# Sorted mixture-of-experts turns in three capacities instead of two, and weight rows laid out four to a partition

## The chip, the cores and the metric

The kernel runs on one core of one Trainium2 chip. The metric is the device time of one launch in microseconds. Three runs of the kernel before took 1242.91, 1248.9 and 1250.15 us (median 1248.9). The one profiled execution took 1235.75 us.

## The reference

Two trunk layers over 384 tokens (128 of context, 256 latent) of width 1024, in float32. Each layer has a mixer (gated linear attention and mLSTM in layer 0, a Hyena long convolution in layer 1), and after it a hierarchical mixture of experts. Only that second half changes here:

```python
g_logits = u @ moe_w_group + b                    # 4 groups, top 1
e_logits = u @ moe_w_router + b                   # 16 experts, top 2 inside the group
hg = einsum('bld,edf->blef', u, moe_w_gate)       # per expert 1024 x 512
hu = einsum('bld,edf->blef', u, moe_w_up)         # per expert 1024 x 512
h  = silu(hg) * hu * gates
out = einsum('blef,efd->bld', h, moe_w_down)      # per expert 512 x 1024
```

Each of the 768 (token, choice) pairs of a layer lands on one of 16 experts. The reference's router, evaluated on its own inputs, gives these counts. Layer 0: experts 0 to 2 have 44, 44, 71; the other thirteen, sorted, 96, 84, 74, 72, 62, 47, 43, 41, 38, 22, 16, 7, 7. Layer 1: 39, 58, 74; sorted 85, 69, 67, 49, 49, 46, 42, 39, 38, 37, 30, 30, 16.

## The kernel before, in words

**Turns.** A layer's mixture is 16 turns `p`, one expert each. Turns 0 to 2 are experts 0 to 2 with room for 96 rows (`CAP`). The other 13 experts are sorted on the chip by their count (L1674 to L1677), and `RANK_AT` says which rank has which turn. Ranks 0 to 5 have 96 rows, ranks 6 to 12 have 64 (`CAP2`). A turn is cut into tiles of 32 rows: 3, 3, 3, then 3, 2, 3, 2, 3, 2, 3, 2, 3, 2, 3, 2, 2, which is 41 tiles a layer. Should an expert have more rows than room, all engines take a slow branch (`over > CAP`) that recomputes every expert; with the counts above neither layer takes it.

**Rows.** VectorE works out the row of each pair (L1674 to L1698), GpSimd scatters the token rows to `x_rows` in HBM (L885) and reads each turn's rows back (L893). The layer's first weights behind the ones loaded ahead are asked for once rows of turn 1 and of turn 2 are in SBUF (L662, L663).

**A tile on TensorE.** `gate_up` (L2258) does 32 matmuls in each of two halves of 16: stationary 128 x 32 (transposed token rows), moving 128 x 256 (128 columns of gate and 128 of up), with four column groups of the array side by side. `hidden_t` transposes the hidden tile of the tile before, `down` (L2284) does 16 matmuls with 256 moving columns for it. A matmul has two records in the profile, so 32 records are one half of `gate_up`, or one `down`. `rows_t` (L2247) transposes the next turn's rows in between. ScalarE and VectorE evacuate and apply silu.

**Weights.** One expert is 2 MB each of gate, up and down, through a ring of slots in SBUF. SyncE's queue issues them (`step`, L654): in step `p`, when the last `gate_up` of turn `p` is done, gate and up of turn `p + 2`, then a down load three turns ahead while `p < AHEAD`, none at `p == AHEAD` (5), and two ahead after it; then `store(p)` writes the turn's results to `y_rows` in HBM. All these go through one hardware queue, in order. Gate and up have contiguous 16 KB of HBM per partition; down is read as `(k p) n`, four separate rows of 4 KB per partition (L426).

**The end of a layer.** In layer 0 TensorE does `first_taps(0)` (L2193, the Hyena filter's first tap; it needs the 1 MB load `w3`, L707 to L710) ahead of the last `hidden_t` and `down`. All results are stored, GpSimd gathers each token's two rows (L903), and they are combined beside the filters (L1570 to L1584 on VectorE, L2205 on TensorE). In layer 1 the last turn stays in SBUF: a selection matrix (`pick`, made by `in_last` and `pick_table`) adds it in a matmul (`last_expert`, L2419), and the gather waits for the stores of turns 0 to 14 only (L900); its second half lands in `uT`, which also holds down weights of every third turn, 14 among them.

Of the kernel before, what the change touches and what calls it, by code (L numbers as in the profile page):

```python
# [35 lines left out]
CAP, CAP2 = 96, 64  # L36
# [3 lines left out]
HALF = RANKS // 2  # L40
AHEAD = 5
RANK_AT = [None] * FIXED + [0, 6, 1, 7, 2, 8, 3, 9, 4, 10, 5, 11, 12]
CAPS = [CAP if r is None or r < HALF else CAP2 for r in RANK_AT]
BASES = [p * CAP if r is None else FIXED * CAP + r * CAP - max(r - HALF, 0) * (CAP - CAP2) for p, r in enumerate(RANK_AT)]
ROWS = sum(CAPS)
TILES = [c // 32 for c in CAPS]
# [64 lines left out]
def build(nc, A, O):  # L111

    ctx = ExitStack()
    with ctx:
# [419 lines left out]
        pick = work[:, 3840:3840 + NT * 2 * P].rearrange("p (j i t) -> p j i t", j=NT, i=2)  # L534
        pick_rows = work[:, 4608:4608 + NT * 2 * P].rearrange("p (j n) -> p j n", j=NT)
# [78 lines left out]
        def _(sp):  # L614
# [18 lines left out]
            def moe_loads(l):  # L633
# [77 lines left out]
                store(NE - 2)  # L711
                if l == 0:
                    store(NE - 1)
# [5 lines left out]
            def overflow_sp(l):  # L719
                sp.wait_ge(S("overflow_flag"), l + 1)  # L720
                over = sp.value_load(flag[0:1, 0:1], min_val=0, max_val=T + CAP - CAP2)
                with sp.If(over > CAP):

                    for i in range(TILES[NE - 1]):
                        evacuated(sp, (l, NE - 1, "Y", i))
# [37 lines left out]
        def _(pool):  # L763
# [113 lines left out]
            def moe(l):  # L877
# [30 lines left out]
                over = pool.value_load(flag[0:1, 0:1], min_val=0, max_val=T + CAP - CAP2)  # L908
# [43 lines left out]
        def _(act):  # L952
# [173 lines left out]
            def moe(l):  # L1126
# [47 lines left out]
                for p in range(1, NE):  # L1174
                    for i in range(TILES[p]):
# [7 lines left out]
                        if i == 1 and l == 1 and p in KEEP_AT:  # L1183
# [3 lines left out]
                        if i == 1 and l == 1 and p in PICK_AT:  # L1187
                            n = PICK_AT.index(p)
                            full(act, ("pick", n))
                            free(act.copy(pick[:, n, :, :], bank(("pick", n))[:, 0:2 * P].rearrange("p (i t) -> p i t", i=2)), ("pick", n))  # L1190
                rows_out(NE - 1, TILES[NE - 1] - 1)
                act.wait_ge(S("overflow_flag"), l + 1)
                over = act.value_load(flag[0:1, 0:1], min_val=0, max_val=T + CAP - CAP2)
# [68 lines left out]
        def _(v):  # L1262
# [355 lines left out]
            def moe(l):  # L1618
# [60 lines left out]
                v.tensor_scalar(small[:, FIXED:], rank, float(HALF), float(CAP - CAP2), ALU.is_ge, ALU.mult)  # L1679
                v.tensor_scalar(base[:, FIXED:], rank, float(CAP), float(FIXED * CAP), ALU.mult, ALU.add)  # L1680
                chain(v.tensor_scalar(late, rank, -float(HALF), 0.0, ALU.add, ALU.max))
                chain(v.scalar_tensor_tensor(base[:, FIXED:], late, -float(CAP - CAP2), base[:, FIXED:], ALU.mult, ALU.add))
# [33 lines left out]
                def in_last(q):  # L1716
                    chain(v.tensor_scalar(here[:, q, :], at2[q], float(BASES[NE - 1]), None, ALU.is_ge))
# [4 lines left out]
                    chain(v.scalar_tensor_tensor(slot[:, q, :], at2[q], -float(BASES[NE - 1]), here[:, q, :], ALU.add, ALU.mult))  # L1722
# [4 lines left out]
                def pick_table():  # L1727
                    chain(v.tensor_tensor(slot[:, 0, :], slot[:, 0, :], slot[:, 1, :], ALU.add))
                    chain(v.tensor_tensor(wl[:, 0, :], wl[:, 0, :], wl[:, 1, :], ALU.add))
                    local = bc(iota[:, 0:2 * 32].rearrange("p (i s) -> p i s", i=2).unsqueeze(2), [P, 2, 4, 32])  # L1730
                    for j in range(NT):
                        v.tensor_scalar(pick_rows[:, j, :].rearrange("p (i q s) -> p i q s", i=2, q=4), local,
# [26 lines left out]
                for p in range(1, NE):  # L1759
                    for i in range(TILES[p]):  # L1760
# [5 lines left out]
                        if i == 1 and p < NE - 1:  # L1766
                            rows_in(p + 1)
# [8 lines left out]
                over = v.value_load(flag[0:1, 0:1], min_val=0, max_val=T + CAP - CAP2)  # L1776
# [115 lines left out]
        def _(pe):  # L1892
# [328 lines left out]
            def moe(l):  # L2221
# [36 lines left out]
                def gate_up(p, i, half):  # L2258
# [67 lines left out]
                for p in range(1, NE):  # L2326
                    for i in range(TILES[p]):
# [7 lines left out]
                        if i == 1 and l == 1 and p in KEEP_AT:  # L2335
# [3 lines left out]
                        if i == 1 and l == 1 and p in PICK_AT:  # L2339
                            n = PICK_AT.index(p)  # L2340
                            pe.wait_ge(S("final_rows"), 1)
                            transposes(("pick", n), [(t * P, pick_rows[:, n, t * P:(t + 1) * P]) for t in range(2)])
# [7 lines left out]
                over = pe.value_load(flag[0:1, 0:1], min_val=0, max_val=T + CAP - CAP2)  # L2350
                with pe.If(over > CAP):
                    for i in range(TILES[NE - 1]):
                        evacuated(pe, (l, NE - 1, "Y", i))
                    with pe.Fori(0, NE * OVF) as n:
# [11 lines left out]
                        for k in range(4):  # L2366
                            ins = pe.transpose(ps[4][:, k * P:(k + 1) * P], hov[:, k * P:(k + 1) * P], ident)
# [180 lines left out]
```

## Time and profile before

| | us |
|---|---|
| median of 3 runs | 1248.9 |
| profiled execution | 1235.75 |
| its span | 1233.9 |
| TensorE matmul busy | 1148.7 (93%) |
| VectorE busy | 377.4 (31%) |
| ScalarE busy | 219.6 (18%) |
| DMA mean rate | 276 GB/s |

The span is 1.85 us shorter than the execution. Busy TensorE is not TensorE at its peak, since matmul records overlap. The mixture's stretches are about 352 to 628 us (layer 0) and 938 to 1212 us (layer 1).

### The profile page before, as it was taken

The numbers are of one execution on the slowest core, as the hardware profiler recorded it, in microseconds if no ns is written. First come the engines' busy times: TensorE is split into PE (matmuls) and PEld (weight loads), VectorE is DVE, ScalarE is ACT, GpSimd is POOL, SyncE is SP. The second block draws the span as 40 slices with busy tenths as digits, with TensorE's granted clock in tenths as the row PEclk, the third lists the DMA queues.
The fourth block names the chain that finished last, engine by engine and source line by source line (L and its number), as shares of the span: only waits on it lengthen the run. The fifth ranks groups of instructions, "written<-read, shape, count | busy, mean of one in ns | idle before, by whom it ended". The sixth has DMA issues, their size and how long they took to land.

```text
span 1233.9 us, 25011 instructions
## 1 busy us (share of the span) xinstructions
PE 1148.7 (93%) x10971; PEld 641.6 (52%) x10971; DVE 377.4 (31%) x962; ACT 219.6 (18%) x465; POOL 141.4 (11%) x163
## 2 busy tenths in 40 slices
PE   5899999899989998988999999999998999998997
PEld 2443445555565554544546665545666555554555
DVE  3201332574341111101157222587624121110114
ACT  2002201321221111111124111121022111111112
POOL 1043100022120000000020000042232000000001
PEclk9899999899999998999999999999999999999999
DMA  9988855359659999999947301001485999999994
GB/s 381 397 299 286 328 201 209 141 166 407 243 208 375 400 403 361 371 399 399 406 141 271 102 36 69 1 0 69 172 354 207 379 398 399 364 374 407 397 371 163
DMA packets 74716, 340.96 MB, mean 276 GB/s; under 512 B 6898, under 2 KB 17681, under 8 KB 59820
## 3 DMA queue, kind: packets, MB, share of 16 engines
q1 hardware_dynamic: 62872, 300.98, 63.0%
q0 software_dynamic: 11248, 37.99, 8.9%
q8 instruction: 88, 1.44, 0.5%
q10 hardware_dynamic: 484, 0.35, 0.1%
q14 instruction: 24, 0.20, 0.1%
HBM read 315.02 MB, written 24.27 MB: 275 GB/s over the span
## 4 chain that ended last, share of the span: by engine, by line
PE 70%; DMA 19%; DVE 5%; issue 2%; ACT 2%; POOL 1%; SPq 1%; POOLq 0%; DVEq 0%; ACTq 0%
PE ps L2272 18%; PE ps L1983 17%; DMA ring<-in_moe_w_up 13%; PE ps L1905 13%; PE ps L2296 6%; PE ps L2496 3%; DMA ring<-in_ada_w 3%; PE ps L1926 3%; PE ps L2205 2%; PE ps L2466 1%; PE ps L1898 1%; PE ps L2255 1%; PE ps L2282 1%; ACT work L1145 1%; DMA x_rows<-work 1%
## 5 line engine op out<-in xcount | busy, mean ns | idle before, releaser
L2272 PE MATMUL ps<-ring,work 128*32 128x256 f32 x5248 | 329.6, 395 | 35.2 <-DMA ring<-in_moe_w_up 31.6
L2272 PEld LDWEIGHTS ps<-ring,work 128*32 128x32 f32 x5248 | 165.7, 113 | 144.1 <-issue 48.4
L1983 PE MATMUL ps<-uT,ring 128*128 128x384 f32 x640 | 214.2, 491 | 2.4 <-DVE uT L1333 1.3
L1983 PEld LDWEIGHTS ps<-uT,ring 128*128 128x128 f32 x640 | 120.2, 191 | 86.4 <-issue 8.0
L2296 PE MATMUL ps<-ring,work 128*32 128x256 f32 x1792 | 106.7, 379 | 0.8 <-DVE work L1751 0.8
L1751 DVE COPY work<-ps 128x128 f32<-128x128 f32 x82 | 23.8, 290 | 254.5 <-PE ps L2282 254.4
L1157 ACT ACTIVATE work<-ps 128x128 f32<-128x128 f32 x82 | 22.8, 278 | 348.2 <-PE ps L2272 348.2
L1905 PE MATMUL ps<-ring,uT 128*128 128x512 f32 x192 | 84.1, 595 | 0.0
L2296 PEld LDWEIGHTS ps<-ring,work 128*32 128x32 f32 x1792 | 57.6, 110 | 39.4 <-DVE work L1751 1.1
L1747 DVE TENSOR_TENSOR work<-ps,work 128x128 f32<-128x128 f32 x82 | 23.9, 291 | 168.7 <-ACT work L1157 168.7
L1836 DVE SCALAR_TENSOR_TENSOR work<-ps,vecT,work 128x127 f32<-128x127 f32 x96 | 35.5, 411 | 91.6 <-ACT work L1240 90.7
L893 POOL DMA_DIRECT2D work<-x_rows x30 | 15.6, 519 | 417.0 <-PE ps L2255 407.2
L1905 PEld LDWEIGHTS ps<-ring,uT 128*128 128x128 f32 x192 | 35.9, 190 | 47.2 <-issue 47.2
L1926 PE MATMUL ps<-ring,silc 128*32 128x512 f32 x384 | 51.2, 668 | 6.4 <-DMA ring<-in_ada_w 5.1
L1163 ACT COPY work<-ps 128x256 f32<-128x256 f32 x82 | 30.5, 372 | 121.9 <-PE ps L2296 121.9
L2496 PE MATMUL ps<-uT,ring 128*128 128x384 f32 x128 | 43.3, 492 | 1.2 <-DVE uT L1883 1.2
L1905 PE MATMUL ps<-work,ring 128*128 128x128 f32 (+3 forms) x256 | 39.7, 293 | 1.5 <-DVE ring L1870 0.8
L1898 PE MATMUL ps<-tab_common,work 128*128 128x128 f32 (+2 forms) x161 | 25.3, 288 | 14.9 <-DMA work<-in_t_pos 11.1
L2296 PE MATMUL ps<-uT,work 128*32 128x256 f32 x624 | 38.4, 379 | 0.0
L1905 PEld LDWEIGHTS ps<-work,ring 128*128 128x128 f32 (+1 forms) x256 | 32.5, 190 | 8.9 <-PE ps L1905 2.5
L931 POOL TENSOR_TENSOR ring<-ring 128x1024 f32<-128x1024 f32 x4 | 13.6, 3403 | 204.1 <-DVE ring L1859 204.1
L1905 PE MATMUL ps<-work 128*128 128x512 f32 x80 | 35.4, 593 | 0.0
(348 smaller groups left out, 1074.4 us busy)
## 6 DMA issues: line engine op xcount, KB each, us to landing
ring<-in_moe_w_gate SPq DMA_DIRECT2D x32, 2048.0 KB, 11.8
ring<-in_moe_w_up SPq DMA_DIRECT2D x32, 2048.0 KB, 16.6
ring<-in_ada_w SPq DMA_DIRECT2D x24, 2048.0 KB, 11.1
ring<-in_moe_w_down SPq DMA_DIRECT2D x22, 2048.0 KB, 19.1
uT<-in_moe_w_down SPq DMA_DIRECT2D x10, 1536.0 KB, 19.4
ring<-in_rec_w_in SPq DMA_DIRECT2D x6, 2048.0 KB, 24.2
ring<-in_hy_w_in SPq DMA_DIRECT2D x6, 2048.0 KB, 11.2
y_rows<-work SPq DMA_DIRECT2D x72, 96.0 KB, 13.6
```

The costliest lines, as they stand in the source:

```text
L1163: free(act.copy(ysb[:, p % 2, i, :], bank((l, p, "Y", i))[:, 0:256]), (l, p, "Y", i))
L1747: free(v.tensor_tensor(hh[:, par, :], bank((l, p, "GU", i))[:, P:2 * P], sg[:, par, :], ALU.mult), (l, p, "GU", i))
L1751: free(v.tensor_copy(hT[:, (FIRST[p] + i) % 2, :], bank((l, p, "HT", i))[:, 0:P]), (l, p, "HT", i))
L1836: ins = v.scalar_tensor_tensor(dst[:, a0 + do:a0 + do + n], src[:, a0 + so:a0 + so + n], w, dst[:, a0 + do:a0 + do + n], ALU.mult, ALU.add)
L1898: ins = pe.transpose(bank(key)[0:n, at:at + p], src, ident[0:p, 0:p])
L1905: ins = pe.matmul(out, lhsT, rhs, start=(i == 0), stop=(i == n - 1))
L1926: ins = pe.matmul(bank(key)[32 * q:32 * q + 32, :], silc[:, 2 * two + k, :], w[:, k, q * 512:(q + 1) * 512], start=(two == 0 and k == 0), ...
L1983: ins = pe.matmul(bank(key)[0:rows, 0:T], w(k), uT[:, k, :], start=(k == 0), stop=(k == DC - 1))
L2205: done(pe.matmul(bank(key)[:], h2T[:, j * P:(j + 1) * P], w3[0:65, at:at + 512], start=True, stop=True), key)
L2272: ins = pe.matmul(bank(key)[32 * q:32 * q + 32, 0:2 * P].rearrange("p (a n) -> p a n", a=2), xg[:, u, k, 32 * i:32 * i + 32], ring[:, 3 * ...
L2296: ins = pe.matmul(bank(key)[32 * q:32 * q + 32, 0:256], hT[:, (FIRST[p] + i) % 2, 32 * k:32 * k + 32], w[:, q * 256:(q + 1) * 256], start= ...
L2496: ins = pe.matmul(bank(("ho", m))[:, 0:T], w[:, k, (m % 4) * P:(m % 4 + 1) * P], uT[:, k, :], start=(k == 0), stop=(k == DC - 1))
```

## The change

Three capacities: ranks 0 to 4 have 96 rows, ranks 5 to 9 have 64, ranks 10 to 12 have 32. The turns' tiles become 3, 3, 3, then 3, 2, 1, 3, 2, 3, 2, 3, 2, 3, 2, 1, 1: 37 a layer. `AHEAD` goes from 5 to 4. In layer 1 the last two turns (one tile each) stay on chip, the gather waits for turns 0 to 13, and its second half lands in ring slot 5. In layer 0 `first_taps(0)` moves behind the last `down`. VectorE gets four more small instructions in the rank arithmetic. The down load takes four consecutive rows per partition (`(p k) n`); the hidden units then have to stand in another order, so each of the four column groups of `gate_up` takes every fourth weight column, a moving operand with a step of 4 float32 (16 bytes).

```diff
-CAP, CAP2 = 96, 64
+CAP, STEP = 96, 32
-AHEAD = 5
-RANK_AT = [None] * FIXED + [0, 6, 1, 7, 2, 8, 3, 9, 4, 10, 5, 11, 12]
+SMALLER = (5, 10)
+AHEAD = 4
+RANK_AT = [None] * FIXED + [0, 5, 10, 1, 6, 2, 7, 3, 8, 4, 9, 11, 12]
+def rank_cap(r):
+    return CAP - STEP * sum(r >= n for n in SMALLER)
+PICKED = (NE - 2, NE - 1)
...
-            return A["moe_w_down"][l, e].rearrange("(k p) n -> p k n", p=P)
+            return A["moe_w_down"][l, e].rearrange("(p k) n -> p k n", p=P)
...
-        last_rows = [utok, uT.rearrange("p k t -> p (k t)").rearrange("p (j d) -> p j d", j=NT)]
+        last_rows = [utok, ring[:, 5, 0:NT * D].rearrange("p (j d) -> p j d", j=NT)]
...
-                store(NE - 2)
                 if l == 0:
-                    store(NE - 1)
+                    for p in PICKED:
+                        store(p)
...
-                        pool.wait_ge(S(f"y{u}_stored"), 4 * 16 * (NE // 2 * (l + 1) - u * l))
+                        pool.wait_ge(S(f"y{u}_stored"), 4 * 16 * (NE // 2 * (l + 1) - l))
...
-                v.tensor_scalar(small[:, FIXED:], rank, float(HALF), float(CAP - CAP2), ALU.is_ge, ALU.mult)
+                v.tensor_scalar(small[:, FIXED:], rank, float(SMALLER[0]), float(STEP), ALU.is_ge, ALU.mult)
+                v.tensor_scalar(above[:, 1, :], rank, float(SMALLER[1]), float(STEP), ALU.is_ge, ALU.mult)
+                v.tensor_scalar(above[:, 2, :], rank, -float(SMALLER[1]), 0.0, ALU.add, ALU.max)
...
+                v.tensor_tensor(small[:, FIXED:], small[:, FIXED:], above[:, 1, :], ALU.add)
+                chain(v.tensor_tensor(late, late, above[:, 2, :], ALU.add))
...
                         for q in range(4):
-                            at = k * DE + q * P
+                            w = ring[:, 3 * u:3 * u + 2, k * DE:(k + 1) * DE].rearrange("p a (n c) -> p a c n", c=4)
                             ins = pe.matmul(bank(key)[32 * q:32 * q + 32, 0:2 * P].rearrange("p (a n) -> p a n", a=2),
-                                            xg[:, u, k, 32 * i:32 * i + 32], ring[:, 3 * u:3 * u + 2, at:at + P],
+                                            xg[:, u, k, 32 * i:32 * i + 32], w[:, :, q, :],
                                             start=(k == 0), stop=(k == DC - 1))
...
+                hidden_t(NE - 1, TILES[NE - 1] - 1)
+                down(NE - 1, TILES[NE - 1] - 1)
                 if l == 0:
                     loaded(pe, "w3")
                     pe.wait_ge(S("sin_out"), 2)
                     first_taps(0)
-                hidden_t(NE - 1, TILES[NE - 1] - 1)
-                down(NE - 1, TILES[NE - 1] - 1)
...
-                    for i in range(2):
-                        evacuated(pe, (l, NE - 1, "Y", i))
+                    for p in PICKED:
+                        evacuated(pe, (l, p, "Y", 0))
                     def last_expert(j):
-                        for i in range(2):
+                        for i, p in enumerate(PICKED):
                             for q in range(4):
...
-                                          ysb[32 * q:32 * q + 32, (NE - 1) % 2, i, :], start=(i == 0), stop=False)
+                                          ysb[32 * q:32 * q + 32, p % 2, 0, :], start=(i == 0), stop=False)
```

## Rows read from the trace of the kernel before

**Rows 1.** The page: busy time of the engines.
```profile
PE 1148.7 (93%) x10971; PEld 641.6 (52%) x10971; DVE 377.4 (31%) x962; ACT 219.6 (18%) x465; POOL 141.4 (11%) x163
```

**Rows 2.** TensorE's waits, 352 to 625 us: engine, line, releaser: total, times, longest.
```profile
PE ps L2272 <- DMA ring<-in_moe_w_up: 16.7, 6, 3.6
```

**Rows 3.** Windows, layer 0: busy us of each engine, TensorE clock, DMA share, GB/s.
```profile
393.00:398.00 5.00, 5.00 (x89) 2.66 (x81) 0.29 (x1) 0.85 (x2) 0.00 (x0) 1.00 1.00 429
402.00:404.00 2.00, 2.00 (x39) 1.12 (x37) 0.29 (x1) 0.00 (x0) 0.00 (x0) 1.00 1.01 410
404.50:407.50 3.00, 3.00 (x64) 1.70 (x54) 0.29 (x1) 0.56 (x2) 0.00 (x0) 1.00 1.04 314
...
490.00:495.00 5.00, 5.00 (x93) 3.02 (x93) 0.58 (x2) 0.65 (x2) 0.00 (x0) 1.00 0.61 168
```

**Rows 4.** Timeline of TensorE, layer 0: start, us, line, instruction, [idle before].
```profile
473.33 3.64 PE L2272 MATMUL ps<-ring,work 128*32 128x256 f32 x32 [3.56 <-DMA ring<-in_moe_w_up]
...
477.31 2.67 PE L2272 MATMUL ps<-ring,work 128*32 128x256 f32 x32
...
591.96 1.93 PE L2272 MATMUL ps<-ring,work 128*32 128x256 f32 x32
...
597.56 1.91 PE L2272 MATMUL ps<-ring,work 128*32 128x256 f32 x32
...
603.64 1.93 PE L2272 MATMUL ps<-ring,work 128*32 128x256 f32 x32
```

**Rows 5.** Timeline of SyncE's queue, layer 0.
```profile
369.49 0.34 SPq L637 DMA_DIRECT2D ring<-in_moe_w_gate  x1
...
607.76 0.57 SPq L630 DMA_DIRECT2D ring<-in_hy_f_w  x1
```

**Rows 6.** DMA issues: what, queue, count, KB each, median us to landing.
```profile
ring<-in_hy_f_w SPq DMA_DIRECT2D x1, 1024.0 KB, 15.3
```

**Rows 7.** The chain of waits, end of layer 0: start, us, what.
```profile
611.90 3.62 PE ps L2272 x32
...
615.77 1.86 PE ps L2272 x32
...
626.53 1.93 PE ps L2296 x32
628.46 1.80 PE ps L2193 x4
630.27 5.35 PE ps L2205 x12
```

**Rows 8.** The chain of waits, end of layer 1.
```profile
1196.31 3.26 PE ps L2272 x32
...
1207.85 0.99 POOL work L903
...
1218.48 1.15 PE ps L2426 x4
```

**Rows 9.** Timeline of VectorE: the rank arithmetic of layer 0.
```profile
348.08 0.17 DVE L1679 TENSOR_SCALAR work<-work 128x13 f32<-128x13 f32 x1
348.17 0.17 DVE L1680 TENSOR_SCALAR work<-work 128x13 f32<-128x13 f32 x1
...
348.44 0.17 DVE L1682 SCALAR_TENSOR_TENSOR work<-work 128x13 f32<-128x13 f32 x1
```

**Rows 10.** Instructions by line, ns min/median/max: small reductions, and copies by ScalarE.
```profile
L1646 DVE TENSOR_REDUCE work<-work x2: 237/238/240, 338.6 to 923.2; 128x12 f32<-128x48 f32 x2
...
L1694 DVE TENSOR_REDUCE work<-work x4: 202/203/203, 351.2 to 936.0; 128x3 f32<-128x48 f32 x4
...
L1145 ACT ACTIVATE work<-ps,work x12: 1115/1134/1159, 337.0 to 925.6; 128x512 f32<-128x512 f32 x12
...
L1119 ACT COPY ring<-ps x24: 567/585/586, 636.5 to 853.0; 128x512 f32<-128x512 f32 x24
```

**Rows 11.** The matmuls of `gate_up` in the same view.
```profile
L2272 PE MATMUL ps<-ring,work x5248: 376/379/637, 352.9 to 1206.9; 128*32 128x256 f32 x195
```

More of the change, by code:

```diff
@@ L39 @@
 RANKS = NE - FIXED
-HALF = RANKS // 2
-AHEAD = 5
-RANK_AT = [None] * FIXED + [0, 6, 1, 7, 2, 8, 3, 9, 4, 10, 5, 11, 12]
-CAPS = [CAP if r is None or r < HALF else CAP2 for r in RANK_AT]
-BASES = [p * CAP if r is None else FIXED * CAP + r * CAP - max(r - HALF, 0) * (CAP - CAP2) for p, r in enumerate(RANK_AT)]
+SMALLER = (5, 10)
[3 more added lines that the diff above has]
+    return CAP - STEP * sum(r >= n for n in SMALLER)
+CAPS = [CAP if r is None else rank_cap(r) for r in RANK_AT]
+BASES = [p * CAP if r is None else FIXED * CAP + sum(rank_cap(n) for n in range(r)) for p, r in enumerate(RANK_AT)]
 ROWS = sum(CAPS)
+PICKED = (NE - 2, NE - 1)
+assert all(CAPS[p] == 32 for p in PICKED) and BASES[PICKED[0]] == ROWS - 64
 TILES = [c // 32 for c in CAPS]
@@ L720, in overflow_sp @@
                 sp.wait_ge(S("overflow_flag"), l + 1)
-                over = sp.value_load(flag[0:1, 0:1], min_val=0, max_val=T + CAP - CAP2)
+                over = sp.value_load(flag[0:1, 0:1], min_val=0, max_val=T + len(SMALLER) * STEP)
                 with sp.If(over > CAP):
-                    for i in range(TILES[NE - 1]):
-                        evacuated(sp, (l, NE - 1, "Y", i))
+                    for p in PICKED:
+                        evacuated(sp, (l, p, "Y", 0))
                     sp.nop().then_inc(S(f"over{l}_y_stored"), 16)
@@ L907, in moe @@
                 pool.wait_ge(S("overflow_flag"), l + 1)
-                over = pool.value_load(flag[0:1, 0:1], min_val=0, max_val=T + CAP - CAP2)
+                over = pool.value_load(flag[0:1, 0:1], min_val=0, max_val=T + len(SMALLER) * STEP)
                 with pool.If(over > CAP):
@@ L1182, in moe @@
                             rows_in(p + 1)
-                        if i == 1 and l == 1 and p in KEEP_AT:
+                        if i == min(1, TILES[p] - 1) and l == 1 and p in KEEP_AT:
                             n = KEEP_AT.index(p)
@@ L1186, in moe @@
                             free(act.copy(x_tok[:, n // 2, n % 2 * 512:(n % 2 + 1) * 512], bank(("xk", n))[:]), ("xk", n))
-                        if i == 1 and l == 1 and p in PICK_AT:
+                        if i == min(1, TILES[p] - 1) and l == 1 and p in PICK_AT:
                             n = PICK_AT.index(p)
                             full(act, ("pick", n))
-                            free(act.copy(pick[:, n, :, :], bank(("pick", n))[:, 0:2 * P].rearrange("p (i t) -> p i t", i=2)), ("pick", n))
+                            free(act.copy(pick[:, n, :, :], bank(("pick", n))[:, 0:len(PICKED) * P].rearrange("p (i t) -> p i t", i=len(PICKED))), ("pick", n))
                 rows_out(NE - 1, TILES[NE - 1] - 1)
                 act.wait_ge(S("overflow_flag"), l + 1)
-                over = act.value_load(flag[0:1, 0:1], min_val=0, max_val=T + CAP - CAP2)
+                over = act.value_load(flag[0:1, 0:1], min_val=0, max_val=T + len(SMALLER) * STEP)
                 with act.If(over > CAP):
@@ L1716, in in_last @@
                 def in_last(q):
-                    chain(v.tensor_scalar(here[:, q, :], at2[q], float(BASES[NE - 1]), None, ALU.is_ge))
+                    chain(v.tensor_scalar(here[:, q, :], at2[q], float(BASES[PICKED[0]]), None, ALU.is_ge))
                     chain(v.tensor_scalar(slot[:, q, :], at2[q], float(ROWS), None, ALU.is_ge))
@@ L1721, in in_last @@
                     chain(v.tensor_tensor((w1, w2)[q], (w1, w2)[q], wl[:, q, :], ALU.subtract))
-                    chain(v.scalar_tensor_tensor(slot[:, q, :], at2[q], -float(BASES[NE - 1]), here[:, q, :], ALU.add, ALU.mult))
+                    chain(v.scalar_tensor_tensor(slot[:, q, :], at2[q], -float(BASES[PICKED[0]]), here[:, q, :], ALU.add, ALU.mult))
                     chain(v.tensor_tensor(here[:, q, :], at2[q], here[:, q, :], ALU.mult))
@@ L1765, in moe @@
                         hidden(p, i)
-                        if i == 1 and p < NE - 1:
+                        if i == min(1, TILES[p] - 1) and p < NE - 1:
                             rows_in(p + 1)
@@ L1775, in moe @@
                 v.wait_ge(S("overflow_flag"), l + 1)
-                over = v.value_load(flag[0:1, 0:1], min_val=0, max_val=T + CAP - CAP2)
+                over = v.value_load(flag[0:1, 0:1], min_val=0, max_val=T + len(SMALLER) * STEP)
                 with v.If(over > CAP):
@@ L2334, in moe @@
                             rows_t(p + 1, i)
-                        if i == 1 and l == 1 and p in KEEP_AT:
+                            if TILES[p] == 1:
+                                rows_t(p + 1, 1)
+                        if i == min(1, TILES[p] - 1) and l == 1 and p in KEEP_AT:
                             n = KEEP_AT.index(p)
@@ L2338, in moe @@
                             transposes(("xk", n), [(m * P, xT[:, 4 * (n % 2) + m, j * P:(j + 1) * P]) for m in range(4)])
-                        if i == 1 and l == 1 and p in PICK_AT:
+                        if i == min(1, TILES[p] - 1) and l == 1 and p in PICK_AT:
                             n = PICK_AT.index(p)
                             pe.wait_ge(S("final_rows"), 1)
-                            transposes(("pick", n), [(t * P, pick_rows[:, n, t * P:(t + 1) * P]) for t in range(2)])
+                            transposes(("pick", n), [(t * P, pick_rows[:, n, t * P:(t + 1) * P]) for t in range(len(PICKED))])
+                hidden_t(NE - 1, TILES[NE - 1] - 1)
+                down(NE - 1, TILES[NE - 1] - 1)
                 if l == 0:
@@ L2366, in moe @@
                         for k in range(4):
-                            ins = pe.transpose(ps[4][:, k * P:(k + 1) * P], hov[:, k * P:(k + 1) * P], ident)
+                            ins = pe.transpose(ps[4][:, k * P:(k + 1) * P], hov.rearrange("p (n c) -> p c n", c=4)[:, k, :], ident)
                         ins.then_inc(S(f"over{l}_ht"), 1)
```

15 lines of the change are left out of this document (8 added, 7 removed).

## The prediction

> **What bounds the kernel now.** I read the page first: TensorE is busy 93% of the span [rows 1], which makes fewer matmuls look like the whole story. Inside a mixture it is not. TensorE's waits show six stops of up to 3.6 us, 16.7 us in all, for the up load in layer 0 [rows 2], and the windows show why: with weights flowing the DMA engines are busy throughout [rows 3]. A tile takes 5.60 us (597.56 less 591.96) and one with a row transpose 6.08 us (603.64 less 597.56) [rows 4]. A pair of turns with five tiles is then about 30 us of TensorE, while its two experts are 12.6 MB, 30 us at 410 to 429 GB/s, and about 1.3 MB of token rows on top, 3 to 4 us. So from the first issue at 369.49 us [rows 5] to the landing of the last up load, at which TensorE starts turn 15 at 611.90 and 1196.31 us [rows 7, 8], the queue of loads sets the pace. I call this landing T. Only what stands behind T is TensorE's and the gather's own.
>
> **Fewer tiles.** Four fewer per layer, eight in all, at 5.60 us are 45 us of TensorE time. Ahead of T nearly all of it turns into longer waits for weights. What is left of it there is traffic: a tile is 32 rows of 4 KB, 0.13 MB read and 0.13 MB written. Four reads and two writes fewer stand ahead of T (the turns up to 13 go from 37 to 35 tiles), 0.79 MB; such rows travel in stretches like 404.5 to 407.5 us, at 314 GB/s [rows 3]: **2.5 us** a layer.
>
> **The gap.** Between 490 and 495 us the rate is 168 GB/s [rows 3], since step 5 issued no down load and the queue ran dry: 5 x (1 - 168/429) = 3.0 us. Now the pause is at step 4, and turn 5 has one tile, so that its slots are free some 12 us sooner and the queue is full when the pause bites. Turn 6 has three tiles and may leave a gap of a microsecond where the queue was short. I take **2.0 us** a layer; bounds 0 and 3.0.
>
> **The down load.** Gate and up (16 KB in a row per partition) run at 429 GB/s, a stretch of down alone (4 KB rows) at 410 [rows 3]. 2.1 MB are 5.11 us at the one and 4.89 at the other, 0.22 us a load; twelve down loads of a layer stand between the first issue and T, 2.7 us, of which I take **2.0**, since the first turns are TensorE's. Below: 0. Above: the stretch where down and token rows mix, 3 us at 314 GB/s, would go at 429 too, 0.8 us more a turn, 9.6 us a layer. I stay near the row of down alone, because that mix contains rows that do not change. The price could be a longer wait of the token rows behind packets four times as long; they are asked for more than a turn before their use, which is the cover.
>
> Together T comes 6.5 us earlier. Layer 1 has the same turns and I take the same: **13.0 us**.
>
> **Behind T, layer 0.** Now turn 15 has two tiles, with `first_taps(0)` between; filters start at 630.27, T + 18.4 [rows 7]. After the change TensorE is through with one tile at about T + 10 (3.6 for the first half and up to 2.7 for the second [rows 4, 7], 1.9 [rows 7] for each of the downs of turns 14 and 15, and some tenths of waiting for VectorE that no other matmul covers any more). But `first_taps(0)` needs `w3`, issued at 607.76 and 15.3 us under way [rows 5, 6], so landed at T + 11.2. It stands behind the last down load in the same queue and comes no sooner against T. From there the taps and three VectorE instructions take about 3 us (an estimate from the 1.80 us of taps [rows 7] and about as much of VectorE), so filters start at T + 14.3: **4.0 us**. The stores and the gather move by more and are no longer last.
>
> **Behind T, layer 1.** The chain runs over down of turn 14, its store, the gather (first at 1207.85, T + 11.5) and ends where TensorE takes the gathered rows, 1218.48, 10.6 us after the gather began [rows 8]. Now the gather needs turn 13's store alone. That is issued ahead of T but queues behind the last down load, 5 us behind T, so it lands at about T + 6.5 and the gather starts at T + 7.3, its rows are there at T + 17.9 instead of T + 22.2: **4.3 us**. TensorE, with a tile less, is there before. Its clock can be low: it will have stood for some 9 us before T, and after a wait of 3.56 us the two halves took 3.64 and 2.67 us [rows 4] against 1.93. These 2.5 us are in the T + 10 above.
>
> **VectorE.** Four more instructions on 128 x 13 values ahead of the row numbers, one of them in the chain: 0.09 us for one that follows the one ahead (348.17 less 348.08), and 0.19 for one in the chain (the 0.27 from 348.17 to 348.44 less one such) [rows 9], 0.46 us a layer, and the scatter, the rows and so the first issue wait for it: **0.9 us lost**. The other edits of constants and the gather's destination cost nothing that a row shows. No turn overflows: the counts of the reference fit 96, 64 and 32, the tightest being 30 in 32.
>
> **The sum.** 13.0 + 4.0 + 4.3 - 0.9 = 20.4 us. The profiled execution would go from 1235.75 to 1215.4. It lies below all three timed runs; on their median of 1248.9 the forecast is **1228 us**.
>
> **The step of four.** This sum takes the strided moving operand at no cost. No matmul of the trace has one. Half a `gate_up` takes 1.86 us on the chain [rows 7] (1.93 in the timeline, which counts the overlap [rows 4]), a record 379 ns [rows 11], with the moving columns in a row. The nearest rows are of other engines: a reduction of 48 values read with a step of 4 takes 238 ns, and 203 with a step of 1, though it also writes 12 values instead of 3; ScalarE's write of 512 values scattered by 512 bytes takes 1134 ns, a plain copy 585 [rows 10]. So the ends are 0 and twice. I take 0 because a float32 matmul goes over its columns slowly: 32 records of 256 columns, four groups side by side, in 1.86 us are 0.9 ns a column and record, so an operand read has that long, and TensorE has slack besides: 37 tiles at 5.60 and 30 row transposes at 0.48 make 222 us in a stretch of 276 (352.9 to 628.46 [rows 7, 11]). An extra microsecond a tile is hidden but for the three tiles ahead of the first issue and the last one.
>
> The Trainium skill speaks against this change here: Advanced Engine Details and Errata, section SBUF Cachelines, says that a 16-byte line wants at least two hits to absorb the SRAM's latency and that a different line on every access costs. A step of 4 float32 is one hit a line. By this rule the sum has a penalty in all 74 tiles, of a size that the page does not state; the rows on VectorE and ScalarE agree with it, none shows it for TensorE.
>
> **Rivals.**
> - *The strided read is slow* (slower than before). Place: all of `gate_up`. If each element costs what the reduction suggests, 35 ns over 48 values or 0.7 ns, a column and record go from 0.9 to 1.6 ns, and a tile's 3.72 us (twice 1.86) become 6.6: 37 x 8.5 + 15 + 5 of waits = 333 us a layer against 276, 57 more, twice: about **1363 us**. At twice the time, 37 x 9.3 + 20 = 364: about **1425**. It decides from `gate_up` about a third longer: (276 - 227)/37 = 1.3 us of 3.72. For it: both rows. Against: the time that a float32 column has. Chance 0.20.
> - *A small cost, mostly hidden.* Half a microsecond to one a tile: 4 exposed tiles a layer, 4 to 8 us lost: about **1234**. Chance 0.08.
> - *T does not move*, because the queue loses its time elsewhere (token rows behind long packets, a gap at turn 6): only the ends count, 7.4 us: about **1241**. For it: the rate dips at every turn to 314. Chance 0.14.
> - *It does not do what it says*: a count over 32 in rank 10 takes the slow branch, far above the range. The margin is two rows. Chance 0.02.
> - The forecast: 0.56, its own range 1214 to 1240 (bounds of down load and gap, and 0.6% between runs).
>
> **How the numbers follow.** About 12 us, 1%, is what can be told from no change here. Faster by more: 0.50 of the forecast's 0.56 and 0.03 of the hidden cost, 0.53. Slower: 0.20, 0.02 and 0.01 for bad luck in the others, 0.23. Within: 0.24. The range is 1210 to 1285: it leaves out the rival of the strided read but for its smallest part, and the overflow, 0.2.
>
> **What would show it.** Half a `gate_up` in a tile without waits: 1.93 us if the step is free. TensorE's waits for the up load grow from 16.7 to over 30 us in layer 0. Turn 15 begins about 6.5 us sooner after the first issue than 242.4 us; no window near 490 us falls under 300 GB/s; 18.4 us from there to the filters become 14, 22.2 us in layer 1 become 18. The prediction is wrong if the 32-record rows read over 2.5 us at full clock, or if waits for loads vanish.

## The result and the profile after

The changed kernel takes 1445.9 us (median), the kernel before 1246.1 in the same comparison: 1.159 times [1.156, 1.162]. The forecast was 1228 us, range 1210 to 1285. What came is the rival "the strided read is slow, at twice", for which I had worked out 1425 us.

The page of the changed kernel: busy time and the costliest group. The group's columns are busy us and mean ns of one record, then idle time before it.

```profile
PE 1377.3 (95%) x10195; PEld 643.8 (45%) x10195; DVE 373.3 (26%) x954; ACT 213.6 (15%) x449; POOL 141.0 (10%) x163
...
L2284 PE MATMUL ps<-ring,work 128*32 128x256 f32 x4736 | 565.1, 632 | 15.1 <-DMA ring<-in_moe_w_up 8.3
```

TensorE has 776 matmul records fewer than before and is busy 229 us longer [rows 1]. One line explains it: a record of `gate_up` takes 632 ns where it took 379 [rows 11]. The timeline of TensorE inside layer 0 shows whole tiles (start, us, what), at full clock:

```profile
660.71 3.80 PE L2284 MATMUL ps<-ring,work 128*32 128x256 f32 x32
...
664.70 3.84 PE L2284 MATMUL ps<-ring,work 128*32 128x256 f32 x32
668.32 1.95 PE L2308 MATMUL ps<-ring,work 128*32 128x256 f32 x32
...
670.59 3.81 PE L2284 MATMUL ps<-ring,work 128*32 128x256 f32 x32
```

Half a `gate_up` is 3.81 us; it was 1.93 [rows 4]. `down` with as many columns, read in a row, stays at 1.95. A tile and its row transpose go from 6.08 us to 9.88 (670.59 less 660.71). The weights no longer set the pace. TensorE's wait for the up load over the whole kernel, then the first issue on SyncE's queue, and the start of turn 15 and of the filters in layer 0:

```profile
PE ps L2284 <- DMA ring<-in_moe_w_up: 8.3, 4, 2.7
```

```profile
374.57 0.33 SPq L645 DMA_DIRECT2D ring<-in_moe_w_gate  x1
```

```profile
711.78 3.82 PE L2284 MATMUL ps<-ring,work 128*32 128x256 f32 x32 [1.49 <-DMA ring<-in_moe_w_up]
...
727.30 5.19 PE L2217 MATMUL ps<-ring,work 65*128 65x512 f32 x7 [0.61 <-DVE ring L1580]
```

From first issue to turn 15 are 337.2 us; before, 242.4 [rows 5, 7]. Of the two signs that were to show the prediction wrong, the first came in full, half a `gate_up` over 2.5 us at full clock, and the second nearly: the waits for the up load fell to 8.3 us over the kernel, from 31.6.

### The profile page after: what moved, and what is told of

The parts are those of the page before. It is cut to its first block, busy times and chain, and to the rows that moved or that the text cites. A ratio compares the mean times of both kernels' runs of the same rounds, so it can differ in the third digit from the quotient of the medians.

```text
span 1443.9 us, 23402 instructions
## 1 busy us (share of the span) xinstructions
PE 1377.3 (95%) x10195; PEld 643.8 (45%) x10195; DVE 373.3 (26%) x954; ACT 213.6 (15%) x449; POOL 141.0 (10%) x163
## 4 chain that ended last, share of the span: by engine, by line
PE 84%; DMA 7%; DVE 5%; ACT 2%; issue 2%; SPq 0%; DVEq 0%; ACTq 0%
PE ps L2284 36%; PE ps L1995 15%; PE ps L1917 10%; PE ps L2308 8%; DMA ring<-in_moe_w_up 4%; PE ps L2510 3%; DMA ring<-in_ada_w 3%; PE ps L2217 2%; PE ps L1938 2%; PE ps L2267 1%; PE ps L2294 1%; PE ps L2480 1%; PE ps L2321 1%; PE ps L1910 1%; ACT work L1153 1%
## 5 line engine op out<-in xcount | busy, mean ns | idle before, releaser
L2284 PE MATMUL ps<-ring,work 128*32 128x256 f32 x4736 | 565.1, 632 | 15.1 <-DMA ring<-in_moe_w_up 8.3
L2308 PE MATMUL ps<-ring,work 128*32 128x256 f32 x1728 | 104.8, 383 | 2.4 <-issue 2.4
L1848 DVE SCALAR_TENSOR_TENSOR work<-ps,vecT,work 128x127 f32<-128x127 f32 x96 | 35.5, 411 | 92.4 <-ACT work L1248 91.6
L1938 PE MATMUL ps<-ring,silc 128*32 128x512 f32 x384 | 48.2, 634 | 6.0 <-DMA ring<-in_ada_w 4.7
L1171 ACT COPY work<-ps 128x256 f32<-128x256 f32 x74 | 27.6, 373 | 113.2 <-PE ps L2308 110.0
L2294 PEld LDWEIGHTS ps<-tab_common,work 128*128 128x128 f32 x74 | 10.3, 139 | 65.1 <-issue 65.1
L1917 PEld LDWEIGHTS ps<-work,ring 128*128 128x128 f32 (+1 forms) x256 | 32.5, 190 | 8.9 <-PE ps L1917 2.5
L1910 PEld LDWEIGHTS ps<-tab_common,work 128*128 128x128 f32 (+2 forms) x161 | 21.8, 166 | 28.5 <-issue 17.2
## 6 DMA issues: line engine op xcount, KB each, us to landing
ring<-in_moe_w_down SPq DMA_DIRECT2D x22, 2048.0 KB, 18.4
```

Source lines behind the costliest of these rows:

```text
L1171: free(act.copy(ysb[:, p % 2, i, :], bank((l, p, "Y", i))[:, 0:256]), (l, p, "Y", i))
L1848: ins = v.scalar_tensor_tensor(dst[:, a0 + do:a0 + do + n], src[:, a0 + so:a0 + so + n], w, dst[:, a0 + do:a0 + do + n], ALU.mult, ALU.add)
L1910: ins = pe.transpose(bank(key)[0:n, at:at + p], src, ident[0:p, 0:p])
L1917: ins = pe.matmul(out, lhsT, rhs, start=(i == 0), stop=(i == n - 1))
L1938: ins = pe.matmul(bank(key)[32 * q:32 * q + 32, :], silc[:, 2 * two + k, :], w[:, k, q * 512:(q + 1) * 512], start=(two == 0 and k == 0), ...
L2294: done(pe.transpose(bank(key)[:, 0:P], hh[:, (FIRST[p] + i) % 2, :], ident), key)
```

## The experiments

All times are medians, beside the kernel before on the same chip (1234.9 to 1236.3 us); ratios are to that. I call "the stretch" the time from the first gate issue of a mixture to the start of turn 15, my T.

**Apart: the sizes alone, the layouts alone, a step of two.** `e1_sizes` is the changed kernel with both layouts as before.

```diff
-            return A["moe_w_down"][l, e].rearrange("(p k) n -> p k n", p=P)
+            return A["moe_w_down"][l, e].rearrange("(k p) n -> p k n", p=P)
...
-            w = ring[:, 3 * u:3 * u + 2, k * DE:(k + 1) * DE].rearrange("p a (n c) -> p a c n", c=4)
...
-            w[:, :, q, :],
+            ring[:, 3 * u:3 * u + 2, at:at + P],
```

> The changed kernel with both layouts taken back: gate and up columns in a row, down as four separate 4 KB rows per partition; three sizes, turn order, on-chip last turns and queue edits stay. Theory A (the strided moving operand alone made the change slow, the rest does what the prediction's sum says): half a gate_up back at 1.93 us, and the time 20.4 - 4 (the down loads' term) = 16 us under the kernel before, about 1230. Theory B (the sizes or the new order cost something too): over 1240, with half a gate_up at 1.93 us all the same.

`e2_layout` is the kernel before with both new layouts (the reverse of these lines).

> The kernel before with the two layouts alone: 41 tiles a layer, step of four, down loads of 16 KB in a row. Theory A: half a gate_up at about 3.7 us as in the changed kernel, a layer's mixture bound by TensorE: 41 x 9.3 + 20 = 401 us against 276, so about 1246 + 250 = 1496. Theory B (part of the 200 us is due to the sizes or the order): under 1450.

`e3_step2` is the changed kernel with a step of two: down rows as two runs of 8 KB.

```diff
-            return A["moe_w_down"][l, e].rearrange("(p k) n -> p k n", p=P)
+            return A["moe_w_down"][l, e].rearrange("(a p c) n -> p a (c n)", a=2, p=P)
...
-            ... .rearrange("p a (n c) -> p a c n", c=4) ... w[:, :, q, :]
+            ... .rearrange("p a (n c) -> p a c n", c=2) ... w[:, :, q % 2, :]
```

> The changed kernel with a step of two: each pair of column groups shares 256 columns and takes every second one, down is loaded as two runs of 8 KB per partition (the part of it that lies apart in three loads instead of two). If the cost goes by hits per 16-byte line (two float32 of a line are used), half a gate_up takes 1.93 us and the time is that of the three sizes alone less 0 to 4 us, about 1228. If any step but one costs: half a gate_up over 2.5 us and the time over 1300.

Measured: sizes alone 1236.7 us, ratio 1.000 [0.998, 1.002]; layouts alone 1505.6 (two runs), 1.217 [1.214, 1.221]; step of two 1242.3, 1.003 [1.001, 1.005]. The group of `gate_up` in the three (sizes, layouts, step of two):

```profile
L2284 PE MATMUL ps<-ring,work 128*32 128x256 f32 x4736 | 298.8, 396 | 71.4 <-DMA ring<-in_moe_w_up 67.2
```

```profile
L2272 PE MATMUL ps<-ring,work 128*32 128x256 f32 x5248 | 627.3, 633 | 9.0 <-issue 6.6 <-ACT work L1152 1.4 <-ACT work L1190 1.0
```

```profile
L2287 PE MATMUL ps<-ring,work 128*32 128x256 f32 x4736 | 309.0, 402 | 67.7 <-DMA ring<-in_moe_w_up 63.6 <-issue 1.9 <-ACT work L1162 1.4
```

So the two layouts together are the whole loss, and there is a second failure: the sizes, worth 16 us in my sum, gave nothing in the median. The step of two met neither of its forecasts (1.93 us and 1228, or over 2.5 us and over 1300). Half a `gate_up` takes 2.01 us, 4% more, and the kernel 5.6 us more than the sizes alone:

```profile
505.40 2.02 PE L2287 MATMUL ps<-ring,work 128*32 128x256 f32 x32
...
507.60 2.01 PE L2287 MATMUL ps<-ring,work 128*32 128x256 f32 x32
```

This run also loads the down weights of every third turn in three pieces instead of two; how much of the 5.6 us is due to that is not separated.

**The price of a step, by itself.** `e4_bench` is the kernel before with matmuls of 512 moving columns added at its start, whose results are not used. Only its groups are read, not its time.

```diff
+            for i in range(16):
+                pe.matmul(ob[:, 0:512], ident, wb[:, 0:2048:4], start=True, stop=True)
...  the same with steps 1, 2, 3, 5 and 8; with 2 of every 8 and 4 of every 8 columns;
...  with 32 stationary columns on four, two and one column groups
```

> The kernel before with extra matmuls at its start, whose results are overwritten: 512 moving float32 columns read from a loaded weight slot with steps 1, 2, 3, 4, 5, 8, then as runs of two in eight and of four in eight; first 16 each on the whole array, then 32 each going round the four column groups; then the stationary operand with a step of four, and steps 1 and 4 on two groups and on one group. Theory A1 (one operand stream pays for each line it touches): on the whole array step 4 takes twice the 595 ns a record of step 1, and so do 5 and 8; step 2 none; one group alone with step 4 pays the same. Theory A2 (four groups reading at once compete for the lines): the whole array and one group alone show no difference between step 1 and 4, four groups do.

The groups (busy us, mean ns). On the full array: step 1, 2, 3, 4, 8, pairs (2 of 8), quads (4 of 8). Then four column groups with steps 1 and 4, and one column group with steps 1 and 4:

```profile
L1999 PE MATMUL ps<-ring,tab_common 128*128 128x512 f32 x32 | 14.0, 595 | 0.9 <-ACT silc L1012 0.9
...
L2001 PE MATMUL ps<-ring,tab_common 128*128 128x512 f32 x32 | 14.6, 611 | 0.0
...
L2003 PE MATMUL ps<-ring,tab_common 128*128 128x512 f32 x32 | 21.8, 847 | 0.0
...
L2005 PE MATMUL ps<-ring,tab_common 128*128 128x512 f32 x32 | 29.0, 1078 | 0.0
...
L2009 PE MATMUL ps<-ring,tab_common 128*128 128x512 f32 x32 | 29.5, 1097 | 0.0
...
L2011 PE MATMUL ps<-ring,tab_common 128*128 128x512 f32 x32 | 14.8, 620 | 0.0
...
L2013 PE MATMUL ps<-ring,tab_common 128*128 128x512 f32 x32 | 13.9, 592 | 0.0
...
L2015 PE MATMUL ps<-ring,tab_common 128*32 128x512 f32 x64 | 7.1, 594 | 0.0
...
L2021 PE MATMUL ps<-ring,tab_common 128*32 128x512 f32 x64 | 14.9, 1098 | 0.0
...
L2037 PE MATMUL ps<-ring,tab_common 128*32 128x512 f32 x32 | 13.9, 592 | 0.0
...
L2041 PE MATMUL ps<-ring,tab_common 128*32 128x512 f32 x32 | 29.0, 1081 | 0.0
```

Busy time is 0.85 ns a column and record with a step of one (14.0 us over 32 x 512), 0.89 with two, 1.33 with three, 1.77 with four, 1.80 with eight. It is the same factor of 2.1 on one column group and on four side by side, so it is not the four groups in each other's way. Pairs 32 bytes apart cost as little as a step of two: what counts is how many elements of one 16-byte line are used, not how far apart the lines are. One element a line doubles the time, two cost 4 to 6% (14.6 and 14.8 us), four cost nothing (13.9). All of it fits one reading, an estimate from these rows: the stream takes the longer of 0.85 ns a column and 1.77 ns a line. A step of two has half a line a column, 0.89 ns; a step of three has three lines for four columns, 1.33 ns. Both are what was measured. The Trainium skill (Advanced Engine Details and Errata, section SBUF Cachelines) has just this rule, at least two hits a line; these rows agree and give it its size for TensorE's float32 stream. And 3.81 us for 1.93 in half a `gate_up` is nearly the same factor, 2.0.

**The down rows without the strided stream.** `e5_dve` keeps the three sizes and the 16 KB down rows. VectorE makes the order of the hidden features with one transpose of 32 x 32 blocks that reads with a step of four; TensorE's transpose of the hidden and the copy out of its bank go. `e8_before_dve` does the same to the kernel before.

```diff
-                                            xg[:, u, k, 32 * i:32 * i + 32], w[:, :, q, :],
+                                            xg[:, u, k, 32 * i:32 * i + 32], ring[:, 3 * u:3 * u + 2, at:at + P],
...
+                    v.transpose(hT[:, par, :].rearrange("p (k t) -> p k t", k=4),
+                                hh[:, par, :].rearrange("p (m k) -> p k m", k=4)).then_inc(S("hT_ready"), 1)
...
-                    free(v.tensor_copy(hT[:, (FIRST[p] + i) % 2, :], bank((l, p, "HT", i))[:, 0:P]), (l, p, "HT", i))
...
-                    done(pe.transpose(bank(key)[:, 0:P], hh[:, (FIRST[p] + i) % 2, :], ident), key)
```

> The changed kernel with its three sizes and its down weights (16 KB in a row per partition) kept, but gate and up columns read in a row again. The order that the down rows need is made by VectorE instead, with a transpose of 32 x 32 blocks that reads the hidden values with a step of four; TensorE's transpose of the hidden and the copy out of its bank go. Theory A (TensorE's strided stream is the whole loss): half a gate_up is back at 1.93 us and the kernel is at the time of the sizes alone, 1237 us. My forecast's term for the down load, 2.0 us a layer, would add 4 us of gain: 1233. Theory B (the 16 KB rows of the down load also slow the mixture, by token rows that wait behind them): above 1245 us. If VectorE's transpose is slow (it stands between every gate_up and its down) TensorE waits for it at every tile, over 0.3 us each, most of it covered by loads.

> The kernel before (two sizes) with the 16 KB rows of down and VectorE's transpose alone. My forecast's term (a down load 0.22 us shorter, twelve a layer): 4 us faster, 1232 us. Theory N (row length is worth nothing, as with 8 KB rows): within 2 us of before, 1236 us. If VectorE's transpose cost TensorE anything on the path, slower by up to 0.3 us a tile, 20 us.

Measured: `e5_dve` 1236.6 us, 1.000 [0.997, 1.002], and `e8_before_dve` 1234.0, 0.999 [0.998, 1.001]. Theory A: take the strided read out of the changed kernel and the ratio falls from 1.159 to 1.000, about 200 us, with the down load as the change has it. (The two medians, 1445.9 and 1236.6, stood beside 1246.1 and 1234.9 for the kernel before, so that not all of their difference is the change's.) VectorE's transpose takes 0.42 us where its copy took 0.29, and nothing on TensorE is seen to wait for it. The group of `gate_up` and the transpose in `e5_dve`:

```profile
L2291 PE MATMUL ps<-ring,work 128*32 128x256 f32 x4736 | 290.0, 401 | 90.1 <-DMA ring<-in_moe_w_up 87.5 <-ACT work L1163 1.4 <-issue 1.2
...
L1766 DVE STREAM_TRANSPOSE work<-work 128x128 f32<-128x128 f32 x74 | 31.2, 422 | 5.0 <-PE ps L2312 2.3 <-DVE work L1762 0.3
```

The 16 KB rows bring nothing that these two can measure.

**Why the sizes gave nothing: the order of turns.** In `e1_sizes` the stretch of layer 0 is still 242.4 us. Three of its views: the first issue and the queue around turn 6, the timeline of TensorE, and the windows there.

```profile
371.48 0.34 SPq L645 DMA_DIRECT2D ring<-in_moe_w_gate  x1
...
449.92 0.38 SPq L645 DMA_DIRECT2D ring<-in_moe_w_down  x1
468.63 1.75 SPq L655 DMA_DIRECT2D y_rows<-work  x4
478.85 0.37 SPq L645 DMA_DIRECT2D ring<-in_moe_w_gate  x1
```

```profile
460.02 3.64 PE L2284 MATMUL ps<-ring,work 128*32 128x256 f32 x32 [13.87 <-DMA ring<-in_moe_w_up]
...
613.86 3.64 PE L2284 MATMUL ps<-ring,work 128*32 128x256 f32 x32 [9.78 <-DMA ring<-in_moe_w_up]
...
625.68 1.02 PE L2205 MATMUL ps<-ring,work 64*1 64x512 f32 x2 [1.17 <-DMA ring<-in_hy_f_w]
...
629.10 5.39 PE L2217 MATMUL ps<-ring,work 65*128 65x512 f32 x12 [0.18 <-issue]
```

```profile
470.00:475.00 5.00, 5.00 (x85) 2.73 (x81) 0.89 (x3) 0.65 (x2) 0.05 (x1) 1.00 0.71 277
475.00:480.00 5.00, 5.00 (x95) 2.80 (x89) 0.70 (x3) 0.28 (x1) 0.46 (x1) 1.00 0.33 87
490.00:495.00 5.00, 4.30 (x76) 2.54 (x68) 0.85 (x2) 0.65 (x2) 0.52 (x1) 1.00 0.99 387
```

The pause of the down loads now falls at step 4. Turn 5, of one tile, is over at once, and TensorE stands 13.9 us for turn 6. When turn 6 starts at 460.0, only what was issued up to 449.9 is on its way; its three tiles hold the slots until 478.85, and the queue has run dry. The gap did close at 490, but one twice as large opened at 470 to 480: 5 x (1 - 277/429) + 5 x (1 - 87/429) = 5.8 us, against the 3.0 us of my sum.

`e6_order` is `e1_sizes` with the turns and the pause where they were before; `e7_order_dve` adds the down rows of `e5_dve`.

```diff
-AHEAD = 4
-RANK_AT = [None] * FIXED + [0, 5, 10, 1, 6, 2, 7, 3, 8, 4, 9, 11, 12]
+AHEAD = 5
+RANK_AT = [None] * FIXED + [0, 6, 1, 7, 2, 8, 3, 9, 4, 10, 5, 11, 12]
```

The two edits go together: no run moves the pause alone.

> The sizes alone, but with the order of turns and the place of the pause as before the change (3, 2, 3, 2, ... with the turns of one tile at 12, 14 and 15). With the new order the stretch from the first issue to the start of turn 15 stayed at 242.4 us in layer 0 and grew by 1.7 us in layer 1, though about 1 MB less was moved. Theory G (the new order costs what fewer bytes gave: turn 6 has three tiles, 18.8 us, behind one expert's load, 15 us, and the queue runs dry at 475 us): the gap falls back to 3 us, these stretches become 240 us, two layers give 4 us: 1233 us. Theory N (the queue would lose it elsewhere): 1237 us, stretch still 242.

> The last two together: three sizes in the old order of turns, 16 KB rows of down, VectorE's transpose of the hidden. If both terms are there, 1229 us; if neither, 1237 us.

Measured: `e6_order` 1229.3 us, 0.994 [0.992, 0.997]; `e7_order_dve` 1224.7, 0.992 [0.990, 0.995]. Both beat the kernel before, by under 1% but with intervals clear of 1, and are the only ones that do. That they come out near the forecast's 1228 us is chance: here the kernel before takes 1234.9, so that the sizes are worth 0.6% and, with the down rows, 0.8%, not the 1.7% of the sum. Of `e6_order` the first issue, turn 15, and the windows at the two places of a gap:

```profile
372.43 0.34 SPq L645 DMA_DIRECT2D ring<-in_moe_w_gate  x1
```

```profile
611.11 3.64 PE L2284 MATMUL ps<-ring,work 128*32 128x256 f32 x32 [8.84 <-DMA ring<-in_moe_w_up]
```

```profile
475.00:480.00 5.00, 3.52 (x33) 1.60 (x33) 0.00 (x0) 0.00 (x0) 0.00 (x0) 0.66 1.02 391
...
490.00:495.00 5.00, 5.00 (x85) 2.91 (x89) 0.90 (x3) 0.65 (x2) 0.52 (x1) 1.00 0.84 308
495.00:500.00 5.00, 5.00 (x96) 2.78 (x88) 0.40 (x2) 0.37 (x1) 0.00 (x0) 1.00 0.92 315
```

At 475 to 480 the rate is 391 GB/s again; the gap is back at 490 to 500 with 5 x (1 - 308/429) + 5 x (1 - 315/429) = 2.7 us.

The stretches of both layers, each from the one profiled execution of its kernel (that of `e6_order` lies 5.7 us below its median, that of `e7_order_dve` 8.3 below, that of `e8_before_dve` 5.9 above):

| kernel | layer 0, us | layer 1, us | ratio to before |
|---|---|---|---|
| before | 242.4 | 241.6 | 1 |
| sizes alone, new order | 242.4 | 243.2 | 1.000 |
| the same, down rows by VectorE | 241.5 | 242.4 | 1.000 |
| sizes alone, old order | 238.7 | 239.5 | 0.994 |
| the same, down rows by VectorE | 236.7 | 237.3 | 0.992 |
| before, down rows by VectorE | 241.8 | 242.0 | 0.999 |

Theory G holds: the new order with its pause cost 3.7 us a layer, and the medians agree (1236.7 against 1229.3 for two layers); G had asked for 4 us in all. The smaller gap is 3.1 us of it (5.8 less 2.7). With the 16 KB rows the stretch is 2.1 us a layer shorter in the old order, near the 2.0 us of my sum, 0.9 in the new one, and in the kernel before not at all over two layers. These three comparisons also take a transpose a tile off TensorE. The intervals of `e6_order` and `e7_order_dve` overlap, so that this term may be small and positive but is not shown.

**From which price on it decides.** In `e9_dose2` and `e10_dose4` two and four of the eight chunks of `gate_up` keep the step of four (`k % 4 == 3` and `k % 2 == 1`), so that the columns of the chunks no longer belong together and only the time can be read; the records of `gate_up` are as many as before, 4736.

```diff
-                                            xg[:, u, k, 32 * i:32 * i + 32], w[:, :, q, :],
+                                            xg[:, u, k, 32 * i:32 * i + 32], w[:, :, q, :] if k % 4 == 3 else ring[:, 3 * u:3 * u + 2, k * DE + q * P:k * DE + (q + 1) * P],
```

> The changed kernel, but only two of the eight chunks of a gate_up (k = 3 and 7) read their columns with a step of four, the other six in a row (gate and up then come out in mixed columns: the product is left wrong). Half a gate_up should take 1.93 + 1.88/4 = 2.40 us, a tile 0.94 us more, 35 us a layer, about what TensorE waits for loads with the sizes alone (35.5 and 31.7 us). Theory M (what the step costs is taken from these waits first, wherever they stand; only the rest and the tiles ahead of the first issue and behind the last load are paid): 1236.7 + 8 = 1245 us. Theory S (each turn takes the longer of its tiles and its load; the eight turns of three tiles are TensorE's already and pay in full, 24 x 0.94 = 22.6 us a layer): 1236.7 + 2 x 24.5 = 1286 us.

> The same with four of the eight chunks (odd k) read with a step of four, the product wrong as before. Half a gate_up 1.93 + 0.94 = 2.87 us, a tile 1.88 us more, 70 us a layer. Theory M: 1236.7 + 2 x (70 - 34) = 1309 us. Theory S: three-tile turns 24 x 1.88 = 45 us, the two-tile turns now just over their load, about 5, and the last tiles 4: 1236.7 + 108 = 1345 us. With all eight chunks M gives 1237 + 2 x (139 - 34) = 1447 us and S about 1469; 1446 was measured.

Measured: 1261.7 us, 1.022 [1.020, 1.024], and 1318.1, 1.069 [1.066, 1.071]. Half a `gate_up` is 2.40 and 2.88 us as expected. A half of each, then the groups of the two:

```profile
502.13 2.40 PE L2284 MATMUL ps<-ring,work 128*32 128x256 f32 x32
```

```profile
505.61 2.88 PE L2284 MATMUL ps<-ring,work 128*32 128x256 f32 x32
```

```profile
L2284 PE MATMUL ps<-ring,work 128*32 128x256 f32 x4736 | 359.7, 448 | 42.4 <-DMA ring<-in_moe_w_up 35.5 <-issue 4.7 <-ACT work L1160 1.4
```

```profile
L2284 PE MATMUL ps<-ring,work 128*32 128x256 f32 x4736 | 428.6, 510 | 31.4 <-DMA ring<-in_moe_w_up 24.6 <-issue 5.4 <-ACT work L1160 1.4
```

Against the sizes alone (298.8 busy, 67.2 waiting) the first adds 60.9 us of matmuls and gives back 31.7 us of waits: 29.2 remain, and the span grew by 29.8. So the first quarter of the price went half into TensorE's 67 us of waits and was paid for the other half. Neither theory's number was met: it is 25 us above the sizes alone where M said 8 and S 49. With four chunks (81 us) it comes near M's 72, S had 108. Where the waits were left is in TensorE's timeline of `e9_dose2`, the only two for loads in layer 0:

```profile
469.58 3.67 PE L2284 MATMUL ps<-ring,work 128*32 128x256 f32 x32 [10.79 <-DMA ring<-in_moe_w_up]
...
628.71 3.67 PE L2284 MATMUL ps<-ring,work 128*32 128x256 f32 x32 [7.49 <-DMA ring<-in_moe_w_up]
```

They are those of turns 6 and 15, each behind a turn of one tile, which has 0.94 us more to fill 13.9 and 9.8 us with. The five shorter waits of layer 0 (35.5 less 13.9 and 9.8, 11.8 us) are gone. That longer three-tile turns also delay the next issue is likely but not shown apart. The decision point of my rival, 1.3 us a tile of free slack, was too generous: 0.94 us a tile already cost 2%.

## Why the prediction was wrong, step by step

**The step of four, taken at 0: the step that failed, about 200 us (a ratio of 1.159 with it, 1.000 without).** I had both ends (0 and twice) and rows on two other engines against it, and still took 0, by an argument that no row showed: that a float32 column of 0.9 ns leaves time for its read. The runs show that the read is not hidden behind it: 0.85 ns becomes 1.77 as soon as each 16-byte line gives one element. The second half of the argument, the slack that 222 us of TensorE leave in 276, is there (with fewer tiles TensorE waited 67 us for loads over both layers), but it is far less than the price: against the sizes alone the matmuls grew by 266.3 us (565.1 less 298.8) and the waits gave back 58.9 (67.2 less 8.3). A smaller price would have been paid as well: of the first quarter's 60.9 us the waits took 31.7. Both nearest rows pointed to a cost. So did the rule of the Trainium skill (Advanced Engine Details and Errata, section SBUF Cachelines). An argument about how fast an engine takes its columns says nothing about how fast they can be read. A chance of 0.20 for it was too little.

**The rival at twice: 1425 us, measured 1446.** 37 x 9.3 + 20 = 364 us a layer was the sum. Measured, from the first `gate_up` (352.1) to the filters (727.30), 375 us. It is made of 37 tiles of 9.42 us (9.88 less 0.46 for the row transpose), 349 us; 14 of row transposes; 4.1 of waits for loads and 3.6 of issue in TensorE's waits of this layer; and 2.8 of the taps, which my 20 us left out. The mechanism of this rival was right, and its size within 1.5%.

**T moves 6.5 us ahead a layer: no.** The rival "T does not move" (0.14) is what the sizes alone did to the stretch; its 7.4 us of gain at the ends are not in the median. The bytes did go (the window over the whole stretch reads 389 GB/s before and 385 after, over the same 242.4 us: about 1 MB less), but the gap, 2.0 us of gain in my sum, became 2.8 us of loss (5.8 for 3.0). I had named the gap at turn 6 and mis-sized it: I counted on a full queue, while a three-tile turn takes 18.8 us and one expert's loads 15. The old order turns the sign: 3.7 and 2.1 us less than before. The down rows' 2.0 us a layer are in no median: 0.9, 2.1 and 0.1 us in the three pairs of stretches. (In the text of the prediction the two times of a down load are also the wrong way round: 5.11 us belongs to 410 GB/s and 4.89 to 429.)

**Behind T.** Layer 0: with the sizes alone filters start 15.2 us after T (629.10 less 613.86), forecast 14.3, before 18.4; a gain of 3.2 for 4.0. The wait for `w3` came where I had put it. Layer 1: the gather starts 6.6 us after T (forecast 7.3), and from T to the end of the span it takes 32.5 us instead of 37.6, 5.1 for 4.3. TensorE no longer waits for gathered rows there; its own chain is last:

```profile
1197.65 3.64 PE ps L2284 x32
...
1208.92 2.01 PE ps L2433 x32
...
1211.16 1.15 PE ps L2440 x4
```

In this execution the two terms came about as forecast. Even so its span is only 3.8 us shorter than before (1230.1 for 1233.9): the first issue of layer 0 came 2.0 us later, 0.44 of it by the rank arithmetic, layer 1's stretch was 1.7 us longer, and 0.8 more went by between the filters of layer 0 and the first issue of layer 1. In the medians nothing is left of it (1236.7 for 1236.3): the profiled execution, 1232.0, is one of the fastest of its twelve, which go up to 1241.2, and where the slower ones lose it was not traced.

**VectorE, 0.9 us lost.** In VectorE's timeline with the sizes alone the rank arithmetic from L1687 (349.32) to L1695 (350.33) takes 1.01 us; before, from 348.08 [rows 9] to 348.65, 0.57: 0.44 a layer, forecast 0.46. The margin of the capacities was misread: the tightest turn is not 30 rows in 32 but the 96 in 96 of layer 0, which the kernel before has as well; no turn overflowed.

**Longer waits for the up load:** 35.5 us in layer 0 with the sizes alone, over 30 as forecast; it says that TensorE has room, not that time was gained. Total, times and longest:

```profile
PE ps L2284 <- DMA ring<-in_moe_w_up: 35.5, 7, 13.9
```

## What to carry to other kernels

A layout that makes a transfer's rows longer moves the stride to whoever reads the tile. Before giving TensorE a strided moving operand count the elements used of each 16-byte line: with four it was free here, with two it cost about 5%, with one every column took twice as long; where the order is needed, let an idle engine make it once on the smaller tensor, as VectorE did here in 0.42 us. And when turns of unequal length share a ring of loads, don't put a short turn ahead of a long one at a moment when the queue holds one expert's loads only: where the short turn and the pause stood decided between no gain and 0.6%.

## What the runs showed of the hardware that was not expected

- The factor for one element a line is 2.1 in busy time on the full array (29.0 against 14.0 us) and the same on a single group of 32 columns; four groups side by side neither hide it nor make it worse (14.9 against 7.1). Beyond a step of four it grows no further (29.5 us with eight).
- A stationary operand with a step of four costs less than a moving one: its load took 308 ns instead of 190, and the matmul's median stayed at 592. The two loads, ns min, median and max, with a step of four and in a row:

```profile
L2031 PEld LDWEIGHTS ps<-ring x32: 307/308/330, 267.0 to 280.1; 128*128 128x128 f32 x32
```

```profile
L2033 PEld LDWEIGHTS ps<-ring x32: 190/190/190, 280.6 to 293.9; 128*128 128x128 f32 x32
```

- Much more waiting went with a lower clock behind it: with the sizes alone the first half `gate_up` after the 13.87 us stop took 3.64 us (nearly twice 1.93: the lower of the two levels), the second 2.43, then 1.93. The mean granted clock was 0.955 there and 0.973 in the kernel before, so that a part of what fewer tiles free is spent at 1.2 GHz. Among the twelve executions with the sizes alone the fastest (1228.95 us) had a mean clock of 0.956 and the slowest (1241.22) 0.948. How much of the run's time the lower level cost was not separated.
